# Eight gate chunks of a two-block transformer kernel: every second low part of their weights moved from GpSimd to VectorE

## The reference, cut to what matters

```python
xn = rms_norm(x, norm_mix_g)
proj = xn @ w_in                      # 1024 -> 2820 columns for the mixers, then 4096 gate columns
y_a = b_gate * short_conv(c_gate * xt)
y_b = spatial gating (gelu, layer norm, causal 128x128 mixing per group)
y_c = stick-breaking attention (4 heads of 64)
y_d = forgetting attention (4 heads of 64, normed q and k)
branches = einsum('bsnc,ncd->bsnd', stack(y_a..y_d), w_branch)
merged = sum(sigmoid(gate_raw) * branches, axis=2)
x = x + merged @ w_out
x = x + swiglu(rms_norm(x))
```

## Time and profile before

| | |
|---|---|
| median of 3 runs | 1125.32 us (1122.8 to 1128.25) |
| the profiled execution | 1122.61 us, of it span of the instructions 1120.8 us |
| TensorE busy | 1022.1 us, 91% of the span |
| VectorE busy | 480.6 us, 43% |
| ScalarE busy | 408.7 us, 36% |
| GpSimd busy | 389.7 us, 35% |
| low parts by GpSimd (L442) | 144 instructions, 360.1 us |
| low parts by VectorE (L442) | 78 instructions, 90.7 us |

### The profile page before, as it was taken

How to read it: one execution, slowest core, us unless ns; L and a number is a source line. 1 busy time by engine, 2 the same in 40 slices (tenths; PEclk the granted TensorE clock), 3 DMA queues, 4 the chain that set the end, 5 groups by cost and what they waited for, 6 DMA issues and landing times.

```text
span 1120.8 us, 13844 instructions
## 1 busy us (share of the span) xinstructions
PE 1022.1 (91%) x5577; PEld 745.7 (67%) x5577; DVE 480.6 (43%) x628; ACT 408.7 (36%) x600; POOL 389.7 (35%) x191
## 2 busy tenths in 40 slices
PE   3998799967999999998899989996989999999994
PEld 3997687745899988987698856664766434444331
DVE  4468322371355435545407417774454122222224
ACT  4444754512554344333454425553233211111001
POOL 4579573833730000002587834446640000000000
PEclk9999899998899999998899999998998999999997
DMA  9545342655665665756254532235687799999960
GB/s 319 189 148 186 112 159 73 218 186 208 199 205 177 237 225 159 261 183 224 80 184 150 188 99 89 75 113 186 253 300 295 298 421 421 422 420 422 420 256 39
DMA packets 84515, 246.60 MB, mean 220 GB/s; under 512 B 4388, under 2 KB 8123, under 8 KB 72031
## 3 DMA queue, kind: packets, MB, share of 16 engines
q1 hardware_dynamic: 82766, 240.47, 58.8%
q0 software_dynamic: 1264, 2.41, 0.9%
q10 hardware_dynamic: 416, 2.77, 0.6%
HBM read 244.59 MB, written 1.05 MB: 219 GB/s over the span
## 4 chain that ended last, share of the span: by engine, by line
PE 80%; DVE 9%; ACT 4%; issue 2%; DMA 2%; POOL 2%; SPq 0%; POOLq 0%; ACTq 0%; DVEq 0%
PE gemm_ps L1217 10%; PE gemm_ps L758 8%; PE gemm_ps L759 7%; PE gemm_ps L760 7%; PE gemm_ps L762 7%; PE gemm_ps L764 7%; PE gemm_ps L763 7%; PE gemm_ps L1248 5%; PE mix_ps L1258 2%; PE gemm_ps L1201 2%; PE mix_ps L758 2%; PE mix_ps L759 2%; PE mix_ps L760 2%; PE gemm_ps L936 1%; DMA ring<-in_w_out_dram 1%
## 5 line engine op out<-in xcount | busy, mean ns | idle before, releaser
L442 POOL TENSOR_TENSOR w_lo<-ring,w_hi 128x1024 fp32r<-128x1024 f32 (+1 forms) x144 | 360.1, 2523 | 423.0 <-ACT w_hi L436 422.9
L436 ACT ACTIVATE w_hi<-ring 128x1024 fp32r<-128x1024 f32 (+2 forms) x222 | 227.2, 1035 | 295.8 <-PE gemm_ps L764 97.1
L758 PE MATMUL gemm_ps<-w_hi,acts 128*128 128x512 f32 (+2 forms) x448 | 179.3, 400 | 27.1 <-POOL w_lo L442 10.4
L762 PE MATMUL gemm_ps<-acts,w_hi 128*128 128x256 f32 x640 | 184.9, 289 | 3.8 <-DVE acts L1729 2.4
L764 PE MATMUL gemm_ps<-acts,w_lo 128*128 128x256 f32 x640 | 181.8, 284 | 0.0
L763 PE MATMUL gemm_ps<-acts,w_hi 128*128 128x256 f32 x640 | 181.7, 284 | 0.0
L759 PE MATMUL gemm_ps<-w_lo,acts 128*128 128x512 f32 (+2 forms) x448 | 174.4, 389 | 0.0
L760 PE MATMUL gemm_ps<-w_hi,acts 128*128 128x512 f32 (+2 forms) x448 | 173.8, 388 | 0.0
L442 DVE TENSOR_TENSOR w_lo<-ring,w_hi 128x1024 fp32r<-128x1024 f32 (+1 forms) x78 | 90.7, 1170 | 107.5 <-ACT w_hi L436 107.3
L762 PEld LDWEIGHTS gemm_ps<-acts,w_hi 128*128 128x128 f32 x640 | 123.5, 193 | 9.3 <-issue 6.5
L763 PEld LDWEIGHTS gemm_ps<-acts,w_hi 128*128 128x128 f32 x640 | 123.5, 193 | 1.3 <-issue 1.2
(11 more groups left out here) (347 smaller groups left out, 1423.9 us busy)
## 6 DMA issues: line engine op xcount, KB each, us to landing
ring<-in_w_in_dram SPq DMA_DIRECT2D x56, 1024.0 KB, 5.2
ring<-in_w_mod_dram SPq DMA_DIRECT2D x24, 1024.0 KB, 5.2
ring<-in_w_ffn_in_dram SPq DMA_DIRECT2D x20, 1024.0 KB, 5.2
late_ring<-in_w_exp_down_dram SPq DMA_DIRECT2D x20, 1024.0 KB, 12.4
late_ring<-in_w_exp_gate_dram SPq DMA_DIRECT2D x18, 1024.0 KB, 12.7
late_ring<-in_w_exp_up_dram SPq DMA_DIRECT2D x18, 1024.0 KB, 10.5
ring<-in_w_ffn_out_dram SPq DMA_DIRECT2D x11, 1024.0 KB, 9.4
ring<-in_w_exp_up_dram SPq DMA_DIRECT2D x9, 1024.0 KB, 11.5
```

Of the source, the lines that this page charges most:

```text
L436: nc.scalar.activation(part(w_hi, u), raw_unit(u), ACT.Copy).then_inc(hi_made, 1)
L442: eng.tensor_tensor(part(w_lo, u), raw_unit(u), part(w_hi, u), ALU.subtract).then_inc(lo_made[unit["maker"]], 1)
L758: mm(dst, xh, wh, start=a_, stop=False, skip_group_check=True)
L762: mm(dst, wh, xh, start=a_, stop=False, skip_group_check=True)
```

## The change

In the gate chunks the maker of units 1 and 3 becomes VectorE; units 0 and 2 stay with GpSimd. VectorE's queue gets eight calls of `lo_up_to`, one for each gate chunk, each behind a step of the mixers. All other makers stay. The semaphores for the landing of the late (expert) weights are replaced by ones that exist already, with the counts that they have by then added to the waits.

```diff
-        maker = None if not split else "dve" if c < 2 or name in ("ffn_g", "ffn_u", "ffn_o") else "pool"
+        by_vector = c < 2 or name in ("ffn_g", "ffn_u", "ffn_o")
...
             for k in range(k0, k0 + kn, per_unit):
...
+                maker = None if not split else "dve" if by_vector or name == "gate" and k // per_unit % 2 == 1 else "pool"
...
-        late_landed = [sem(f"late_landed{slot}") for slot in range(LATE_RING)]
-        first_landed = [sem(f"first_landed{slot}") for slot in range(FIRST)]
+        in_ring = [len([i for i in range(len(pieces)) if i % RING == r]) for r in range(RING)]
+        late_landed = [sem(f"late_landed{slot}") for slot in range(LATE_RING - RING)] + landed
+        landed_earlier = [0] * (LATE_RING - RING) + in_ring
+        first_landed = [sem("ws_in"), sem("vec_rows")]
+        first_earlier = [1, len(ROWS)]
...
-                eng.wait_ge(first_landed[f], 16)
+                eng.wait_ge(first_landed[f], 16 * (first_earlier[f] + 1))
             else:
-                eng.wait_ge(late_landed[(f - FIRST) % LATE_RING], 16 * ((f - FIRST) // LATE_RING + 1))
+                slot = (f - FIRST) % LATE_RING
+                eng.wait_ge(late_landed[slot], 16 * (landed_earlier[slot] + (f - FIRST) // LATE_RING + 1))
...
             link(V_.tensor_scalar(fs[:, 8:16], fflat, 0.0, None, ALU.min))
+            lo_up_to(units_of[index["gate"][0]][-1])
...
             dve.wait_ge(sem("stick_z"), 1)
             V_.tensor_scalar(T1, PM[:, :, 0:384], HD ** -0.5, None, ALU.mult).then_inc(sem("stick_z_read"), 1)
             dve.wait_ge(sem("stick_z_read"), 1)
             link(V_.tensor_scalar(T3, T1, 0.0, None, ALU.max))
+            lo_up_to(units_of[index["gate"][1]][-1])
             dve.wait_ge(sem("stick_ln"), 1)
             link(V_.tensor_tensor(T3, T3, T2, ALU.add))
...
             link(V_.tensor_tensor(T1, T1, tab("strict_neg").unsqueeze(1).to_broadcast([P, 4, 384]), ALU.add))
+            lo_up_to(units_of[index["gate"][2]][-1])
             dve.wait_ge(sem("fox_ln"), 1)
...
             V_.tensor_copy(NLF.rearrange("p t h n -> p (t h) n"), fs[:, 0:8].unsqueeze(2).to_broadcast([P, 8, P])).then_inc(sem("fox_f"), 1)
+            lo_up_to(units_of[index["gate"][3]][-1])
             dve.wait_ge(sem("stick_c"), 1)
             V_.tensor_tensor(T1, T1, PM[:, :, 0:384], ALU.subtract).then_inc(sem("stick_logw"), 1)
+            lo_up_to(units_of[index["gate"][4]][-1])
...
             V_.nop().then_inc(sem("stick_o_read"), 1)
+            lo_up_to(units_of[index["gate"][5]][-1])
...
             V_.tensor_scalar(fs[:, 24:32], fs[:, 24:32], -1.0, None, ALU.mult).then_inc(sem("fox_max"), 1)
+            lo_up_to(units_of[index["gate"][6]][-1])
             dve.wait_ge(sem("fox_e"), 8)
...
             V_.tensor_tensor(T2[:, :, P:384], T2[:, :, P:384], fs[:, 36:40].unsqueeze(2).to_broadcast([P, 4, 2 * P]), ALU.mult).then_inc(sem("fox_p"), 1)
+            lo_up_to(units_of[index["gate"][7]][-1])
             dve.wait_ge(sem("fox_p_turned"), 1)
```

## The result

The changed kernel takes 1145.77 us in the median of four runs (1143.59 to 1146.19), the kernel before 1124.55 beside it (1122.8 to 1128.25): ratio 1.0173, 95% interval 1.0154 to 1.0191, so 21 us slower by the medians and 17 to 21 by the interval. The profiled execution took 1146.19 us, its span is 1144.4, 23.6 longer than before. Lines of the code have moved: what was L442 (low part) is L447, L436 (high part) L441, L758 is L763, L893 is L898; in VectorE's mixer steps the shift is 5 to 13.

The account below looks back on a forecast made before the run. TensorE was taken to bound the kernel (80% of the chain), GpSimd's rate ending none of its three gate waits. Losses 2.4 + 2.1 + 4.4 + 0.4 + 5.1 + 1.5 + 1.7 = 17.6 us on 1122.6 gave 1140, range 1132 to 1149.

Parts of the forecast that it names:

- Gate 2, the largest term: Gate chunk 2: low parts behind L1825 to L1827 leave TensorE standing after unit 0, from 119.0 to 130.05; loss 4.4 us.
- nothing more: Clock after gate 2's stand: 11.1 us takes the place of 6.66, so no further slow-clock loss.
- Gate 5: Gate chunk 5: VectorE's low part stands behind two mixers' output and loses a turn to GpSimd; 5.1 us, otherwise 2.9.
- Gate 0: Gate chunk 0: low part stands behind the fox norm, VectorE free at 95.45, TensorE waits until 96.7; loss 2.4 us.
- 2.4 and 2.1 are like the 2.44: Clock after the new stands in gates 0 and 1: like the old 2.44 us stand, no slow clock follows.
- Gate 1: Gate chunk 1: low part comes behind L1821 and L1823 (1.76 and 1.75 us), at 109.0, wanted at 106.97; loss 2.1 us.
- Gate 6: Gate chunk 6: old 2.44 us stand goes, but `fox_p` comes late, twice waiting for GpSimd; 1.5 us lost.
- The clock: TensorE's halved clock after long stands: only gate 5's stand adds a new slow stretch, 1.7 us in the sum.
- Absorption: Behind the gate stage: the loss vanishes where the experts' loads keep the DMA engines at 0.91; no change, 1125; chance 0.04.
- a gain: Branch sums: GpSimd done earlier, so VectorE's six sums no longer take turns with it; 8.3 us faster, 1114; chance 0.03.
- Rival 1: Races between VectorE and GpSimd: turns fall to VectorE or cost it little; 10.9 us slower, 1133.5; chance 0.25.
- GpSimd and VectorE take turns: Shared SBUF access: instructions exclude each other whole, first to issue winning; L1807 took 2.53 us for 0.43 of work.

Follow-up runs that it names:

- gate5_sooner: The changed kernel with the low part of gate 5.1 made ahead of the second branch's split in VectorE's queue; 1139.58 us, ratio 1.0124 to the kernel before.
- gate2_alone: The kernel before with only units 1 and 3 of gate chunk 2 moved to VectorE; 1129.73 us, ratio 1.0053 to the kernel before.
- gate2_back: The changed kernel with gate chunk 2's low parts given back to GpSimd; 1139.95 us, ratio 1.0155 to the kernel before.
- gate0_alone: The kernel before with only units 0 and 1 of gate 0 made by VectorE, ahead of its wait for the root; 1118.51 us, ratio 0.9951.

## Why the prediction was right

It said 1140 us (1132 to 1149) and slower with 0.93; measured 1145.8. The mechanism was the one forecast, gate by gate. The sizes fit less well than the total, as the points on gate 1 to 3 and on the clock show.

- **Gate 2, the largest term.** Predicted: TensorE stands 11.1 us before unit 1 and comes back with two units more to do. Found: 10.64, and 11.12 when gate 2 alone is moved. Gates 1 to 3 together 6.4 us against 6.5, but by two errors that cancel: gate 1 was 0.85 too high (below), and "nothing more" for the clock behind this stand was too low. TensorE ran at half its clock until 140.6 in place of 135.0, 5.6 us in place of 3.9, so 0.9 us more.
- **Gate 5.** Predicted: the race with GpSimd is lost by 0.2 us, 5.1, and a slow stretch, 1.7. Found 6.5 for both, and the race undone by gate5_sooner.
- **Gate 0.** The stand is right (2.22 for 2.4), and so is VectorE's freedom at 95.06 (95.45). Mis-sized: the step "2.4 and 2.1 are like the 2.44" in the clock's part. The 2.2 us stand, five microseconds behind the one of 3.1, was followed by a slow stretch of its own (0.50 at 97 to 99), so the part cost 3.8.
- **Gate 1.** 1.25 for 2.1: I gave L1823 its 1.75 us of before, which it had beside GpSimd; alone it took 0.96 (L1829 in the trace after). The correction of durations that I made for L1807 should have been made here too.
- **Gate 6.** 2.11 us of stand at the transposes with two waits for GpSimd in L1880 and L1881 (2.71 and 3.31 us for 0.69 and 1.23 of work), as forecast; 1.0 lost for 1.5.
- **The clock** is the term that was mis-sized most: 1.7 in the sum, about 6 in the trace (an estimate, half the time at 0.50): 1.7 in gate 0, 0.9 in gate 2, 1.7 in gate 5, 1.6 at the transposes. The step "2.4 and 2.1 are like the 2.44" judged by the length of the stand alone, and the runs show that this doesn't decide: behind 2.44 us before gate 6.3 the clock was 1.00 in the kernel before and 0.50 in gate2_alone, behind 2.1 us at the transposes 0.50 in the changed kernel and 1.00 in gate2_back and gate5_sooner.
- **Left out:** 1.7 us between the transposes and the branches (the slow clock at 220), and 3.7 behind them. These two are most of the distance between the 17.6 of the sum and the 23.6 of the profiled execution. By the medians the distance is 3.6.
- **The rivals.** Absorption and a gain were wrong: the stretch behind is not shorter, and the branch sums still take turns with GpSimd (1.86, 2.09, 2.06, 2.05 and 2.05 us; five times in either kernel, not six as the prediction has it). Rival 1 (VectorE wins) is what gate5_sooner makes of gate 5.
- **"GpSimd and VectorE take turns"** held at L1807, at gate 5 and at `fox_p`. As a rule it is too simple, see the last section.

## What to carry to other kernels

When work is moved from one in-order queue to another, compute for each moved instruction when its new engine gets to it and when its reader wants it: 16 instructions of 1.2 us cost 21 us behind the wrong waits and nothing, within 3 us, in front of them. Put the piece that is wanted first in front of the wait that it doesn't depend on, and look for pieces that stand behind something foreign in the old queue: two such low parts brought 5.5 us by the ratio of gate0_alone (2.4 in its trace). When one of two engines that exclude each other from memory gets less to do, give the other's instructions their undisturbed durations before working out when it arrives.

## What the runs showed of the hardware that I had not expected

An instruction of VectorE that waits for GpSimd isn't sure of the next turn. In gate0_alone, VectorE's and then GpSimd's timeline:

```profile
90.58 12.96 DVE L1811 TENSOR_TENSOR arena<-arena,st 128x1024 f32<-128x1024 f32 x1
```

```profile
88.09 14.37 POOL L447 TENSOR_TENSOR w_lo<-ring,w_hi 128x1024 fp32r<-128x1024 f32 x6
103.27 2.56 POOL L447 TENSOR_TENSOR w_lo<-ring,w_hi 128x1024 fp32r<-128x1024 f32 x1 [0.81 <-ACT w_hi L441]
```

The product, 1.23 us for this shape alone (L1869 in the earlier trace rows), stood for 12.96, while GpSimd made six low parts in 14.37 us, 2.40 each, four of them begun after VectorE's instruction; it got through only in the gap of 0.81 us at 102.5. In the trace before the same instruction beside the same kind of work took 3.39. The Trainium skill (SBUF — State Buffer, section "Who interferes with whom") says that whoever issues first gets the shared ports for the whole instruction; by that VectorE, issued at 90.58, would have gone ahead of the low part that GpSimd began at 92.87, and this run shows that it did not. What decides between a turn and six in a row stays open. It cost something too: VectorE came late to the scores, and TensorE stood 3.88 us before the transposes behind gate 1.
